# Two attention layers of a fused kernel: local heads moved beside the token products, the first output units run between the other heads

## What is computed

```python
for l in range(2):
    h = rmsnorm_2(x, norm_g[l])
    proj = h @ w_in[l]              # a_q a_k a_v a_g | b_cq b_ckv b_kr b_g | c_q c_k c_v c_g
    ya = swa_attention(a_q, a_k, a_v, sink, positions)   # 8 "local" heads of 128, window, ALiBi, sink
    yb = mla_attention(b_cq, b_ckv, b_kr, ...)           # 4 "latent" heads: q, k, v made from norms of b_cq, b_ckv
    yc = diff_attention(c_q, c_k, c_v, ...)              # 4 heads, each of two softmaxes of 64 (8 "diff" jobs)
    y = concat([ya * silu(a_g), yb * silu(b_g), yc * silu(c_g)])   # 8 + 4 + 4 blocks of 128 channels
    x = x + y @ w_out[l]
return rmsnorm_2(x, final_norm)
```

## Time and profile before

| | us |
|---|---|
| median of 3 runs | 2373.35 (2368.74 to 2374.34) |
| span of the profiled execution | 2372.3 |
| TensorE matmuls busy in it | 2273.5 |
| VectorE busy | 1363.0 |
| ScalarE busy | 1055.6 |
| GpSimd busy | 57.7 |
| layer 1 of 2: end of `c_vg` / end of group 0 of `out` | 1750.8 / 1855.7 |
| layer 2 of 2: the same | 2190.3 / 2295.8 |

### The profile page before, as it was taken

How to read it: one execution, slowest core, us unless ns; L and a number is a source line. 1 busy time by engine, 2 the same in 40 slices (tenths; PEclk the granted TensorE clock), 3 DMA queues, 4 the chain that set the end, 5 groups by cost and what they waited for, 6 DMA issues and landing times.

```text
span 2372.3 us, 31751 instructions
## 1 busy us (share of the span) xinstructions
PE 2273.5 (96%) x13038; PEld 1973.5 (83%) x13038; DVE 1363.0 (57%) x1694; ACT 1055.6 (44%) x1366; POOL 57.7 (2%) x66
## 2 busy tenths in 40 slices
PE   8999989899989999999999999999998999999898
PEld 7888978787877888888888887888976889898676
DVE  5545656475566666766766444644456454444654
ACT  5433443423455545454555333533445443343543
POOL 0000020011000000000000000000000000000000
PEclk9999998899999999999999999999999999999999
DMA  8556520013634555555565556555531556564033
GB/s 282 193 168 221 178 88 1 1 32 139 202 127 137 190 183 193 179 193 183 189 205 187 194 195 197 195 185 183 170 99 36 178 176 221 162 202 161 1 125 141
DMA packets 235977, 373.07 MB, mean 157 GB/s; under 512 B 8359, under 2 KB 108244, under 8 KB 235092
## 3 DMA queue, kind: packets, MB, share of 16 engines
q1 hardware_dynamic: 229740, 362.89, 46.3%
q10 hardware_dynamic: 6120, 8.50, 1.0%
HBM read 369.25 MB, written 2.12 MB: 157 GB/s over the span
## 4 chain that ended last, share of the span: by engine, by line
PE 64%; DVE 5%; issue 5%; ACT 2%; POOL 0%; DVEq 0%; POOLq 0%; ACTq 0%
PE PS L465 16%; PE PS L424 12%; PE PS L426 12%; PE PS L425 12%; PE PS L468 8%; PE PS L1941 1%; PE PS L1925 1%; DVE w_lo L342 1%; ACT w_hi L337 1%; DVE small L1979 1%; DVE spare L1975 1%; PE PS L904 1%; ACT spare L1953 0%; DVE h_both L921 0%; PE PS L2608 0%
## 5 line engine op out<-in xcount | busy, mean ns | idle before, releaser
L342 DVE TENSOR_TENSOR w_lo<-raw,w_hi 128x2048 fp32r<-128x2048 f32 (+2 forms) x340 | 766.4, 2254 | 766.5 <-ACT w_hi L337 766.2
L337 ACT ACTIVATE w_hi<-raw 128x2048 fp32r<-128x2048 f32 (+2 forms) x340 | 641.2, 1886 | 842.4 <-PE PS L426 487.4
L465 PE MATMUL PS<-h_both,w_hi 128*128 128x512 f32 x1968 | 539.4, 395 | 2.9 <-DVE h_both L921 1.8
L424 PE MATMUL PS<-w_hi,h_both 128*128 128x512 f32 (+2 forms) x1344 | 511.6, 381 | 11.3 <-DVE h_both L921 4.6
L425 PE MATMUL PS<-w_lo,h_both 128*128 128x512 f32 (+2 forms) x1344 | 508.3, 378 | 0.0
L426 PE MATMUL PS<-w_hi,h_both 128*128 128x512 f32 (+2 forms) x1088 | 408.7, 376 | 0.0
L465 PEld LDWEIGHTS PS<-h_both,w_hi 128*128 128x128 f32 x1968 | 336.6, 189 | 49.5 <-DVE h_both L921 2.8
L468 PEld LDWEIGHTS PS<-h_both,w_lo 128*128 128x128 f32 x1968 | 302.1, 189 | 42.1
L468 PE MATMUL PS<-h_both,w_lo 128*128 128x256 f32 x1968 | 313.1, 281 | 0.0
L424 PEld LDWEIGHTS PS<-w_hi,h_both 128*128 128x128 f32 x1344 | 255.3, 190 | 59.8 <-DVE h_both L921 5.1
L425 PEld LDWEIGHTS PS<-w_lo,h_both 128*128 128x128 f32 x1344 | 255.1, 190 | 45.8
(11 more groups left out here) (508 smaller groups left out, 2027.1 us busy)
## 6 DMA issues: line engine op xcount, KB each, us to landing
raw<-in_w_in SPq DMA_DIRECT2D x132, 1024.0 KB, 5.2
raw<-in_ffn_w_up SPq DMA_DIRECT2D x176, 512.0 KB, 4.4
raw<-in_w_out SPq DMA_DIRECT2D x48, 1024.0 KB, 5.1
raw<-in_ffn_w_down SPq DMA_DIRECT2D x44, 1024.0 KB, 5.1
raw<-in_mem_wkv SPq DMA_DIRECT2D x8, 1024.0 KB, 11.6
raw<-in_mem_wq SPq DMA_DIRECT2D x4, 1024.0 KB, 5.3
raw<-in_mem_wo SPq DMA_DIRECT2D x4, 1024.0 KB, 7.0
raw<-in_w_in SPq DMA_DIRECT2D x4, 768.0 KB, 4.7
```

The lines of the kernel that those rows point to most:

```text
L337: act.activation(w_hi[:, slot % 2, :st.n], raw[:, slot, :st.n], ACT.Copy).then_inc(hi_made, 1)
L342: dve.tensor_tensor(w_lo[:, slot % 2, :st.n], raw[:, slot, :st.n], w_hi[:, slot % 2, :st.n].bitcast(F32), ALU.subtract).then_inc(lo_made, 1)
L424: pe.matmul(ps, l_hi, r_hi, start=start, stop=False, skip_group_check=skip)
L465: pe.matmul(sums, wh[:, k, cs], h_both[:, :, kk, :], start=kk == 0, stop=False, skip_group_check=True)
```

## The change

- The 8 local heads leave the lanes. They run on 4 lanes of their own (PSUM banks 4 to 7), two to a lane, woven among the units of `tok` and `tok_end`: `local_tensor`, `local_scalar`, `local_vector`. The silu of a_g moves with them, one half in round 6, the other in round 10 of `tok`.
- `out` unit 0 is rounded in the first round of the heads and multiplied in two halves of the tokens (`multiply_rows`) in rounds 6 and 8. Unit 1 follows in round 14, unit 2 by halves in rounds 16 and 18; unit 3 comes behind the heads.
- The lanes of the diff jobs use slot 1 of `w_hi` and `w_lo` for their scratch; two start in round 0, two in round 2. All 4 latent heads start in round 13 and wait there for `latents` and for all diff jobs.
- Turned blocks go through PSUM banks 7 and 5.

```diff
+        def multiply_rows(pe, q, j, t, ready=None):
+            st, bank, slot = q.st, 2 * q.parity + t, (q.first + j) % 2
...
+            pe.wait_ge(lo_made, q.unit(j + 1))
...
+            for k in range(st.kb):
+                kk = j * st.kb + k
+                last = three_pass(pe, PS[:, bank, :st.n_cols], h_hi[:, kk, t * P:(t + 1) * P], h_lo[:, kk, t * P:(t + 1) * P],
+                                  wh[:, k, :], wl[:, k, :], kk == 0, kk == st.units * st.kb - 1)
+            if t == TB - 1:
+                last.then_inc(unit_used, 1)
...
+        def local_scalar(act, j):
...
+            yield
+            yield
+            yield
+            act.wait_ge(j.dve, j["neg1"])
...
+            act.activation(j.lane["ex"], nm, ACT.Exp, bias=job["sink"]).then_inc(j.act, 1)
+            yield
+            yield
+            act.wait_ge(j.pe, j["turned"])
+            act.activation(s_, PS[:, bank, :], ACT.Copy).then_inc(j.act, 1)
...
+        def beside_products(part, e, layer):
+
+            made = L2[layer]["local"]
+            return together(*[one_by_one([rounds(n + 1)] + [part(e, j) for j in js]) for n, js in enumerate(made)])
...
+        def local_gates_scalar(act, layer):
+            g, st = L2[layer]["gates"], ST2[layer]["tok"]
+            for n in range(2):
+                yield from rounds(6 if n == 0 else 4)
...
+                g_ = ztok[:, :, AG + 512 * n:AG + 512 * (n + 1)]
+                act.activation(g_, g_, ACT.Silu).then_inc(g.act, 1)
...
             for job in mla[1:]:
-                job["idle"] = 3
...
-            SWA, DIFF_, MLA = 1, 9, 17
-            picks = [[SWA + 6, DIFF_ + 0, DIFF_ + 4], [SWA + 7, DIFF_ + 1, DIFF_ + 5], [0, MLA], [SWA, SWA + 1, MLA + 1],
-                     [DIFF_ + 2, DIFF_ + 6], [DIFF_ + 3, DIFF_ + 7], [SWA + 2, SWA + 3, MLA + 2],
-                     [SWA + 4, SWA + 5, MLA + 3]]
-            return on_lanes(jobs, picks, starts)
+                job["idle"] = LATENT_ROUNDS
...
+            DIFF_, MLA = 1, 9
+            for n in (2, 3):
+                diff[n]["idle"] = 2
+            picks = [[DIFF_ + n, DIFF_ + 4 + n] for n in range(4)] + [[0, MLA], [MLA + 1], [MLA + 2], [MLA + 3]]
+            return on_lanes(jobs, picks, starts, late_lanes)
+
+        LATENT_ROUNDS = 13
...
+        MIXED_BANKS = (7, 7, 7, 7, 7, 5, 7, 5)
...
         def mixed_tensor(pe, layer, j):
...
+            q = Group(ST2[layer]["out"], 0)
+            yield
+            local_made(pe, layer)
+            for n in range(4):
                 mixed_turn(pe, j, n)
...
+                yield
+                if n == 2:
+                    multiply_rows(pe, q, 0, 0, ready=lambda: pe.wait_ge(j.dve, j["lo1"]))
+                if n == 3:
+                    multiply_rows(pe, q, 0, 1)
+                yield
+            yield from rounds(5)
+            d = L2[layer]["diff"]
+            for t in range(TB):
+                multiply_rows(pe, q, 1, t, ready=lambda: pe.wait_ge(j.dve, j["lo3"]))
+            yield
+            pe.wait_ge(d.dve, d["n11"])
+            for n in (4, 5):
                 mixed_turn(pe, j, n)
             yield
+            multiply_rows(pe, q, 2, 0, ready=lambda: pe.wait_ge(j.dve, j["lo5"]))
+            yield
+            yield
+            multiply_rows(pe, q, 2, 1)
+            yield
...
         def mixed_scalar(act, layer, j):
...
+            q = Group(ST2[layer]["out"], 0)
+            split_hi(act, q, 0)
+            yield
+            yield
+            for n in range(4):
                 mixed_hi(act, j, n)
...
+                yield
+                yield
+            yield from rounds(3)
+            diff_made(act, layer)
+            split_hi(act, q, 1)
+            yield
+            yield
+            yield
+            for n in (4, 5):
                 mixed_hi(act, j, n)
+            split_hi(act, q, 2)
             yield
...
         def mixed_opening_tensor(pe, layer, j):
...
             lanes_made(pe, lanes2[layer])
...
             for n in (6, 7):
                 mixed_turn(pe, j, n)
...
+            multiply(pe, Group(ST2[layer]["out"], 0), 3, ready=lambda: pe.wait_ge(j.dve, j["lo7"]))
             yield
 
         def mixed_opening_scalar(act, layer, j):
...
             lanes_made(act, lanes2[layer])
...
             for n in (6, 7):
                 mixed_hi(act, j, n)
...
+            split_hi(act, Group(ST2[layer]["out"], 0), 3)
...
-                for name in ("kv", "tok", "tok_end"):
-                    run(products_tensor(pe, st[name]))
+                run(products_tensor(pe, st["kv"]))
+                fill = beside_products(local_tensor, pe, layer)
+                weave(products_tensor(pe, st["tok"]), fill)
+                weave(products_tensor(pe, st["tok_end"]), fill)
+                run(fill)
```

More of the change, by code:

```diff
@@ L1922, in head_tensor @@
                 wait_latents(pe, job["layer"])
+                diff_made(pe, job["layer"])
             for t_ in range(TB):
@@ L2368, in gates_scalar @@
             yield
[L2369 to L2375, removed]
+            yield
+            yield
+            act.wait_ge(act_evac, ST2[layer]["tok_end"].G1)
+            act.wait_ge(dve_evac, ST2[layer]["tok_end"].G1)
+            g_ = ztok[:, :, BG:BG + 512]
+            act.activation(g_, g_, ACT.Silu).then_inc(g.act, 1)
+            yield
             yield
@@ L2446, in ranks_scalar @@
                     act.wait_ge(places.act, places["sin"])
+                    for js in L2[layer]["local"][2:]:
+                        act.wait_ge(js[-1].pe, js[-1]["mixed"])
                 act.activation(ar(QR, wd), ztok[:, 0, c0:c0 + wd], ACT.Square,
@@ L2525, in put @@
                 h = j.job["h"]
+                if j.job["name"] == "swa" and t_ == 0:
+                    g = L2[j.job["layer"]]["gates"]
+                    dve.wait_ge(g.act, g[f"g{h // 4}"])
                 g_ = ztok[:, t_, g0 + h * P:g0 + (h + 1) * P]
@@ L2741, in mixed_scalar @@
             yield
         def mixed_vector(dve, layer, j):
-            for _ in range(MIXED_ROUND):
+            q, ssq, d = Group(ST2[layer]["out"], 0), L2[layer]["ssq"], L2[layer]["diff"]
+            split_lo(dve, q, 0)
+            yield
+            yield
+            for n in range(4):
+                mixed_lo(dve, j, n)
                 yield
-            ssq, d = L2[layer]["ssq"], L2[layer]["diff"]
+                yield
+            yield from rounds(3)
             for job in L2[layer]["diff_heads"]:
@@ L3106, in _ @@
                 run(products_scalar(act, st["kv"], before=end_of(st["q"]), more=True))
-                run(products_scalar(act, st["tok"], before=end_of(st["kv"]), more=True))
-                run(products_scalar(act, st["tok_end"], before=end_of(st["tok"]), more=True))
+                fill = together(local_gates_scalar(act, layer), beside_products(local_scalar, act, layer))
+                weave(products_scalar(act, st["tok"], before=end_of(st["kv"]), more=True), fill)
+                weave(products_scalar(act, st["tok_end"], before=end_of(st["tok"]), more=True), fill)
+                run(fill)
                 fill = together(gates_scalar(act, layer), ranks_scalar(act, layer))
@@ L3199, in _ @@
                 run(products_vector(dve, st["kv"], before=end_of(st["q"]), more=True))
-                run(products_vector(dve, st["tok"], before=end_of(st["kv"]), more=True))
-                run(products_vector(dve, st["tok_end"], before=end_of(st["tok"]), more=True))
+                fill = beside_products(local_vector, dve, layer)
+                weave(products_vector(dve, st["tok"], before=end_of(st["kv"]), more=True), fill)
+                weave(products_vector(dve, st["tok_end"], before=end_of(st["tok"]), more=True), fill)
+                run(fill)
                 fill = together(gates_vector(dve, layer), ranks_vector(dve, layer))
```

228 lines of the change are left out of this document (134 added, 94 removed).

## The result

The changed kernel takes 2385.61 us (median of 4, 2382.54 to 2386.25) against 2373.36 for the kernel before: 1.0055 times as long, 95% interval 1.0041 to 1.0070. The forecast was 2385. Run again on another chip (the run called after2) it took 2390.52 us against 2372.93 there, 1.0077 (1.0062 to 1.0092). Its profiled execution has a span of 2383.3 us, 11.0 more than before.

What follows compares the result with a forecast made beforehand. TensorE, busy 96% of the span, was taken as the bound. Work 68.2, stalls 21.5 and moved heads 17.9 make 107.6 against 105.2 us, +2.4 a layer; with clock 3.5, two layers add 11.8 to 2373.35: 2385 us, range 2368 to 2399.

Steps and rivals of the forecast that it cites:

- Local heads, 17.9 us: `tok` and `tok_end`: eight local heads at 2.24 us of TensorE lengthen them by 17.9 us a layer.
- the 0: `tok` rounds with silu and exponentials: no added wait for late rounding, 0 us taken, bounds 0 to 3 a layer.
- rival 3: `tok`: silu and exponential rounds delay rounding, TensorE waits for `w_lo`, 10 us in all, 2395 us; chance 0.15.
- Stalls, 21.5 us: Behind `c_vg`: TensorE waits per layer, summed from start, rounds 2, 5, 13, 16 and unit 3; bounds -2 and +3 us.
- round 2: Start of the heads: first transposes wait 5.2 us, as unit 0's rounding precedes the first distance bias.
- round 5: Heads: diff jobs 4 and 5 wait 2.1 us for results of 0 and 1, behind `mixed_lo` on VectorE.
- B: Stretch from the end of `c_vg` to the end of group 0 of `out`: 89.7 us forecast before the clock term.
- an estimated 0.65 us: Round 0: `split_lo` of unit 0 delayed by POOL's silu product through memory exclusion, 0.65 us more a layer.
- The clock, 3.5 us: Behind the three stalls over 5 us: half-clock stretches of 3.4 us cost 3.5 us a layer; bounds 0.5 and 7.
- Rival 1: No measurable change: stalls as counted, clock falls only while TensorE stands; 5.8 us or less, 2376 to 2379; chance 0.23.
- Rival 2: Faster: local heads cost TensorE less between units, at half the price 2367 us; chance 0.10.
- the 19.1 us of before: Stretch behind `c_vg` before the change: 105.2 - 86.1 us of TensorE standing or at slow clock.

Runs made afterwards that it cites:

- warm: Changed kernel with all three TensorE waits of 5.2 to 5.4 us filled with 44 identity transposes each, schedule unmoved: 2378.36 us, 1.0018.
- localonly: Local heads run among the units of `tok`; lanes, order and `out` units as in the kernel before, turned pairs four rounds earlier: 2361.53 us, 0.9954.
- three: Changed kernel with the edits of late0, early2 and early3 together: 2373.08 us, 1.0002.
- best: Changed kernel with ahead0, early2, early3, turned pairs 4 and 5 behind unit 1, unit 2's second half behind pairs 6 and 7: 2348.81 us, 0.9904.
- late0: Changed kernel with unit 0 of `out` rounded in round 3 of the heads instead of round 0: 2392.31 us, 1.0080.
- early2: Changed kernel with unit 2 of `out` rounded in round 14 instead of round 16: 2379.13 us, 1.0021.
- early3: Changed kernel with unit 3 of `out` rounded in round 17 instead of behind turned pairs 6 and 7: 2383.14 us, 1.0048.
- ahead0: Changed kernel with unit 0 of `out` rounded ahead of the heads, behind the last unit of `c_vg`: 2373.33 us, 1.0010.
- dummy: Changed kernel with 44 identity transposes only in the third wait, before unit 3 of `out`: 2384.53 us, 1.0053.
- late0fill: late0 with 12 identity transposes meant to fill the wait before the latent heads' scores; they ran behind it: 2389.90 us, 1.0071.

## Why the prediction was right, and where it was not

**Direction and size.** Forecast +11.8 us, measured +12.3 and, on the second chip, +17.6. The account by layer is 18.2 + 95.8 - 105.2 = 8.8 us, twice 17.6, where the prediction had 5.9. So the closeness of 2385 to 2385.61 is partly luck: one term was too small by 2.6 us a layer, and the first profiled execution had 13.7 us less half clock in unchanged parts than that of before, and 6.9 less than that of after2, so that its section began 5.2 and 3.8 us earlier.

**Local heads, 17.9 us.** Measured 18.2 (201.0 - 182.8, both at full clock). TensorE has no wait among `tok` and `tok_end`, and the one at the start of `c_qk`, 1.81 us for `w_lo`, is as long as before the change: the 0 was right, and rival 3 did not occur. ScalarE where the first silu comes, in order of time:

```profile
1610.13 1.28 ACT L2499 ACT_TABLE_LOAD   x1
1611.42 1.06 ACT L2499 ACTIVATE arena<-arena 128x1024 f32<-128x1024 f32 x1
1615.44 1.91 ACT L338 ACTIVATE w_hi<-raw 128x2048 fp32r<-128x2048 f32 x1 [2.96 <-PE PS L427]
```

The rounding behind it does not come late: ScalarE stood 2.96 us for its slot. The load starts 0.02 us behind the end of the rounding ahead of it (1608.20 + 1.91 = 1610.11), and the silu 0.01 us behind the end of the load. By the figure of the Trainium skill, "ScalarE: Activation LUTs", "What ACT_TABLE_LOAD costs", an estimated 1.38 us of drain would come on top of the load; this trace shows none on either side of it, and the 2.96 us would have covered it.

**Stalls, 21.5 us.** warm shows them at full clock. Start 1.06 (forecast 1.1); round 2 5.38 (5.2), second head 1.2 (1.1); round 5 1.6 (2.1); round 13 1.4 (1.1); unit 2 5.3 (5.6); unit 3 5.2 (5.35). Their sum is 21.2, and B is 89.7 as forecast. The first transposes came 10.83 us behind `c_vg`, not at 10.35. The prediction had put an estimated 0.65 us on a conflict between `split_lo` and POOL, outside its sum, and something of that size is there: in after, `split_lo` of unit 0 takes 2.90 us, from 1769.01, instead of the 2.29 of the earlier trace rows, and POOL's product runs from 1767.26 to 1769.78. No run took POOL's product away. For the rest, this is what following the rounds of each engine gave, from prices of before alone.

**The clock, 3.5 us.** This term was mis-sized: it measured 6.1 us a layer (95.8 - 89.7). The earlier trace rows has 3.4 us at half clock behind a wait of 2.5 us, and I took one such slice for each stall. At stalls of 5.2 to 5.4 us it was 6.8 us each time in the changed kernel, in both layers and in both executions. The two behind units 2 and 3 cost about 2.4 each (5.29 - 2.86 for half a unit; 4.7 for the third in two layers) where 1.5 was taken; behind round 2, 1.2 is left of 7.2 / 2 = 3.6, where 0.5 was. The upper bound of 7, two such slices each, was nearer than the middle value. Rival 1, by which the clock falls only while TensorE stands, is refuted by warm: the waits as long, the time 12.2 us less.

**Rival 2** fell as it was put: between units the heads have no discount. Yet the faster side was nearer than the prediction saw. It took the 19.1 us of before as belonging to the stretch and not to the heads that leave it. localonly shows that 3.7 and 5.1 us a layer of them go with the local heads. In the account by A and B, which leaves the unchanged parts out, the move alone is worth -6.8 us (-10.7 by the medians of one chip), and the new order of what stays costs 16.3 + 6.8 = 23.1, or 24.0 by after2. three, which moves the rounding of units 0, 2 and 3 and nothing else, gives 10.5 us a layer of B back (95.8 - 85.3). best gives back 20.4; it rounds unit 0 ahead of the heads and also changes TensorE's order. So the loss lies in where units are rounded and multiplied and in the clock that goes with the waits, and not in the move or in the late latent heads, which best keeps. No run tells how much of the second 10 us is rounding and how much TensorE's order.

**My expectations of the first repairs** were too hopeful for another reason: a rounding moved to a new round stands in front of something else there. late0 gave back 3.7 of 5 us to the second diff scores; in early2 and early3 2.1 us were left, since `mixed_lo` itself lies right in front of the product that needs it. Only best, which also changes TensorE's order, has no wait for a turned pair's low part.

## What to carry to other kernels

A move onto a full engine is priced twice: by its own work, which adds one to one, and by what its absence does to the waits it leaves; where a round is paced by another engine, an item that leaves it gives back that engine's pace (1.77 us for a local head here, read from rows) and not its own 0.44. When work is reordered, follow each engine's queue past the moved rounding or copy, and place it where its input has long been there and nothing due is queued behind it (`ahead0`). Look at the chain of the end stretch by stretch before calling an engine the limit: here it showed 14 us of VectorE in a program with TensorE busy 96% of the span. Count a wait of TensorE of over 5 us at its length and 1.2 to 2.4 us on top, as in warm, the most where products stand behind it; if it can't be removed, transposes that nobody reads gave that part back.

## What the runs showed of the hardware

- At each idle time of TensorE of 5.2 to 5.4 us, from start to start, the changed kernel had 6.8 us at 1.2 GHz, which began between 2.3 us before the wait ended and 0.2 us behind its end; the 2.5 us in before came with 3.4. Over all kernels, 33 of 38 such idle times had 6.8 us; the others had 3.4 (early2 and late0) or 10.2 (early3 and dummy). The length of a wait alone does not tell it: before has 6.8 us at the start of the heads, where no wait is over 1.1 us. With the three waits filled by transposes of the identity the granted clock stayed 1.00.
- In late0, 17.1 us at half clock came while TensorE was busy with scores, in one layer and not in the other. Three of the four executions took 2392 to 2395 us and one 2383.48, so it may be frequent there; late0fill had it in no layer. Open.
- The half clock in unchanged parts differs between executions of kernels that are the same up to there (at 457 us, 20.5 us in one piece or 10.3 in two). Two medians on different chips differed by 5 us (2385.61 and 2390.52 for one kernel, with before at 2373.36 and 2372.93), and ten executions of early2 on one chip by 12 us. Whether the chip plays a part is not shown. Gains of that size need the stretch itself, or many runs on a common chip.
